# First mixer: queries and keys projected with head dimensions on the partitions

## The chip, the cores and the metric

The program runs on one NeuronCore of a Trainium2 chip. The metric is the device time of one execution, in microseconds (us), the median of a few runs. It computes two transformer blocks one after the other in f32 for 512 tokens of width 1024. The change lies in the first block's mixer, which is the first fifth of the span.

## The reference

The mixer projects the normalised input and turns queries and keys by a rotary angle, per head of 64 dimensions, in two halves of 32:

```python
proj = jnp.einsum('bsd,de->bse', xn, w_in)
q_a, k_a, v_a, q_r, k_r, v_r, g_r, gate_logits = jnp.split(proj, IN_SPLIT_POINTS, axis=-1)

def apply_rotary(t, cos, sin):
    t1, t2 = jnp.split(t.astype(jnp.float32), 2, axis=-1)
    return jnp.concatenate([t1 * c - t2 * s, t1 * s + t2 * c], axis=-1)
```

There are 24 attention heads, in 3 groups of 8. Group 0 attends in a window of neighbouring tokens, groups 1 and 2 with dilations 4 and 16, so their tokens are taken apart by their place modulo 4. The three groups' outputs are mixed by a softmax over their log-sums. Beside attention there are 8 retention heads (queries and keys of 64, values of 128, a gate g_r through silu) and 16 blocks of 128 gate logits through a sigmoid. The attention part and the retention part, each through its own branch matrix, are gated, added and projected; after that come a mixture of 64 experts and the whole second block, which the change doesn't touch.

## The kernel before, in words

SBUF holds one arena. `m.aT` is the normalised input with the model dimension on the partitions: 8 slices `m.aT[:, k, :]` of 128 x 512 tokens. Weights come in 28 chunks into a ring of three slots (`m.ring`), loaded by SyncE in the order of use.

The list `STEPS` sets the order of the whole mixer; every engine walks through it. A step projects one piece into one of two PSUM banks, `banks[s % 2]`, in turn:
- "A" (48 steps: 4 head pairs q, 3 groups g, 4 token tiles t): 128 tokens of queries, keys and values of two heads, 384 columns, as 8 matmuls over k. The stationary operand is a slice of `m.aT` of 128 tokens, for dilated groups every fourth token (`m.aT[:, k, t::4]`); the moving operand is the weight, 384 wide (line 429).
- "R1" and "R2" (32 steps): the same for two retention heads: queries, keys and the first head's values; then the second head's values and both gates.
- "G" (16 steps): 128 gate logits, with the weight stationary and all 512 tokens moving (line 425).

Of an A or R1 step, ScalarE copies the values out. Queries and keys lie there with tokens on the partitions: VectorE multiplies by cosine and sine (lines 629 to 631), GpSimd adds (line 752), and one step later TensorE turns the result by two transposes (line 438), which ScalarE copies to `m.qk` or `m.rqk` (line 544).

Between projections stand units, two for each head pair, at the steps in `UNITS`: an attention unit makes scores (line 450), VectorE masks them and takes maxima, ScalarE the exponentials (line 554) one step later, TensorE transposes them two steps later (line 472, copied by line 564) and multiplies them by the values three steps later (line 484). A retention unit makes scores (line 463), VectorE multiplies them by a table of decays that GpSimd made (lines 760 and 761, line 669), TensorE multiplies by the values one step later (line 498), and VectorE and GpSimd normalise and gate.

An engine waits by counting semaphores: `proj_done` counts finished projections, `proj_read` and `rope_read` the reads that let a bank be used again, `qk_ready` the finished queries and keys. Every engine executes in the order of its own loop, so a wait holds up all that stands behind it.

SyncE's queue carries, besides the chunks, the reorder of attention outputs through DRAM and an exchange of retention queries and keys between partition halves (`m.rqs`). It issues in order: a wait ahead of one transfer delays all later ones. The weights of later stages stand behind those of the mixer.

Of the kernel before, what the change touches and what calls it, by code (L numbers as in the profile page):

```python
# [7 lines left out]
ALU = mybir.AluOpType  # L8
# [3 lines left out]
P = 128  # L12
# [45 lines left out]
def constants():  # L58

    p = np.arange(P)[:, None]  # L60
    c = np.arange(WB)[None, :] - WOFF
    t = {}
    t["ident"] = np.eye(P)
    inv = (1.0 / (np.float32(10000.0) ** (np.arange(0, HD, 2, dtype=np.float32) / np.float32(HD)))).astype(np.float32)
    ang = (np.arange(S, dtype=np.float32)[:, None] * inv[None, :]).astype(np.float32)
    cos, sin = np.cos(ang.astype(np.float64)), np.sin(ang.astype(np.float64))
    t["cos"] = cos.reshape(T, P, HD // 2).transpose(1, 0, 2).reshape(P, -1)
    t["sin"] = sin.reshape(T, P, HD // 2).transpose(1, 0, 2).reshape(P, -1)
    t["nsin"] = -t["sin"]
    for name in ("cos", "sin"):  # L70
        x = cos if name == "cos" else sin
        t[name + "4"] = x.reshape(P, T, HD // 2).reshape(P, -1)
    t["nsin4"] = -t["sin4"]
# [98 lines left out]
MIX_STEPS = {12 * (q + 1) + 14: q for q in range(4)}  # L172


def chunk_no(s):

    return s // 4 if s < 80 else 20 + (s - 80) // 2
# [4 lines left out]


def rope_steps():
    return [s for s, x in enumerate(STEPS) if x[0] in ("A", "R1")]
# [45 lines left out]
def mixer_memory(arena):  # L231
# [3 lines left out]
    m.cos, m.sin, m.nsin = (sp(T, HD // 2) for _ in range(3))  # L235
    m.cos4, m.sin4, m.nsin4 = (sp(T, HD // 2) for _ in range(3))
    m.trig = Space(arena, at)(6 * T * HD // 2)
# [17 lines left out]
    m.ra = [sp(4, 2, HD // 2) for _ in range(2)]  # L255
    m.rb = [sp(4, 2, HD // 2) for _ in range(2)]
    m.rot = [sp(2 * HP2) for _ in range(2)]
# [34 lines left out]
    "proj_done", "rope_read", "rot_ready", "proj_read", "t_done", "qk_ready", "s_done",  # L292
# [54 lines left out]
def first_of_mixer(sp, A, m, G):  # L347

    consts = A["consts"]
    cols, _ = const_columns()  # L350
    for t in range(T):
        sp.wait_ge(G[f"x_in{t}"], 16)
    for i, name in enumerate(("ret_decay_fwd", "ret_decay_bwd")):
        sp.dma_start(m.decay[:, i, :], A[name][0].partition_broadcast(P)).then_inc(G["tables_in"], 16)
    sp.dma_start(m.trig, consts[:, cols["cos"][0]:cols["cos"][0] + 6 * T * HD // 2])\
# [11 lines left out]
def sp_mixer(sp, A, m, G, by_token):  # L367
    need = Need(sp)
    for c in range(N_CHUNK):
        if c < NSLOT:  # L370
            continue
        if c >= NSLOT:
# [12 lines left out]
            if c % 2 == 0 and 0 <= hp < 4:  # L385
                need(G["qk_ready"], 48 + 4 * (hp + 1))
                need(G["s_done"], ATT_BANKS * len(ATT_UNITS))
                if hp >= 2:
# [12 lines left out]
ROPES = [s for s, x in enumerate(STEPS) if x[0] in ("A", "R1")]  # L401


def ropes_to(s):

    return sum(r <= s for r in ROPES)

# [5 lines left out]
def pe_mixer(nc, pe, m, G, banks):  # L413
    need = Need(pe)
    for s in range(NSTEP):

        if s < NPROJ:
            kind, a, b, t = STEPS[s]
# [3 lines left out]
            w = m.ring[c % NSLOT]  # L422
            for k in range(KT):
                if kind == "G":
                    ins = pe.matmul(banks[s % 2][:, :], w[:, k, tile(b)], m.aT[:, k, :],
                                    start=(k == 0), stop=(k == KT - 1))
                else:
                    rows = m.aT[:, k, t::4] if kind == "A" and b else m.aT[:, k, tile(t)]
                    ins = pe.matmul(banks[s % 2][:, 0:CW], rows, w[:, k, :],  # L429
                                    start=(k == 0), stop=(k == KT - 1))  # L430
            ins.then_inc(G["proj_done"], 1)

        if s - 1 in ROPES:
            n = ROPES.index(s - 1)
            need(G["rot_ready"], n + 1)
            need(G["qk_ready"], n)
# [17 lines left out]
        if u and u[0] == "ret":  # L454
            _, hp, k, _ = u
            r, rows = RET_UNITS.index(u), slice(RK * k, RK * k + RK)
            need(G["qk_ready"], 48 + 4 * (hp + 1))
# [18 lines left out]
        if u and u[0] == "att":  # L476
# [3 lines left out]
            need(G["proj_read"], 12 * (q + 1))  # L480
# [9 lines left out]
        if u and u[0] == "ret":  # L490
# [4 lines left out]
            need(G["proj_read"], 48 + 8 * (hp + 1))  # L495
# [7 lines left out]
def act_mixer(nc, act, A, m, G, banks):  # L503
    need = Need(act)
    step = Tick(act, G["act_step"])
    for s in range(NSTEP):
        if s < NPROJ:
            kind, a, b, t = STEPS[s]
            bank = banks[s % 2]
            need(G["proj_done"], s + 1)  # L510
            if kind in ("A", "R1"):
                need(G["rope_read"], ropes_to(s))
            if kind == "A":
                need(G["pv_done"], 2 * (a - 1))
                act.activation(m.v[a % 2][:, t, b, :], bank[:, 2 * HP2:3 * HP2], ACT.Copy)\
                   .then_inc(G["proj_read"], 1)
            if kind == "R1":
                need(G["ro_done"], 2 * (a - 1))
                act.activation(m.rv[a % 2][:, t, tile(0)], bank[:, 2 * P:3 * P], ACT.Copy)\
                   .then_inc(G["proj_read"], 1)  # L520
            if kind == "R2":
                need(G["ry_ready"], 2 * (a - 1))
                act.activation(m.rv[a % 2][:, t, tile(1)], bank[:, 0:P], ACT.Copy)
                act.activation(m.rg[a % 2][:, t, :], bank[:, P:3 * P], ACT.Silu)\
                   .then_inc(G["proj_read"], 1)
# [7 lines left out]
        if s - 1 in ROPES:  # L533
            n = ROPES.index(s - 1)
            kind, a, b, t = STEPS[s - 1]
            need(G["t_done"], n + 1)
            src = banks[2][:, 0:2 * P].rearrange("p (i c) -> p i c", i=2)
            if kind == "A":
                need(G["s_done"], 2 * ATT_BANKS * (a - 1))
                dst = m.qk[a % 2][:, b, :, tile(t)]  # L540
            else:
                need(G["rs_done"], 8 * (a - 1))
                dst = m.rqk[a % 2][:, :, tile(t)]
            act.activation(dst, src, ACT.Copy).then_inc(G["qk_ready"], 1)
# [47 lines left out]
def dve_mixer(nc, dve, m, G, banks):  # L592
# [23 lines left out]
    for sn in range(NSTEP):  # L616

        if sn < NPROJ and sn in ROPES:
            n = ROPES.index(sn)
            t = STEPS[sn][3]  # L620
            x = banks[sn % 2][:, 0:2 * HP2].rearrange("p (h two d) -> p h two d", h=4, two=2)
            need(G["proj_done"], sn + 1)
            need(G["rot_ready"], n - 1)
            by4 = STEPS[sn][0] == "A" and STEPS[sn][2] > 0
            cos, sin, nsin = (m.cos4, m.sin4, m.nsin4) if by4 else (m.cos, m.sin, m.nsin)
            cos = cos[:, t, :].unsqueeze(1).unsqueeze(1).broadcast_to([P, 4, 2, HD // 2])
            sin = sin[:, t, :].unsqueeze(1).broadcast_to([P, 4, HD // 2])
            nsin = nsin[:, t, :].unsqueeze(1).broadcast_to([P, 4, HD // 2])
# [113 lines left out]
def pool_mixer(nc, pool, A, m, G):  # L742
# [4 lines left out]
    for s in range(NSTEP):  # L747
        if s < NPROJ and s in ROPES:
            n = ROPES.index(s)
            need(G["rope_read"], n + 1)  # L750
            need(G["t_done"], n - 1)
            pool.tensor_tensor(m.rot[n % 2], m.ra[n % 2].rearrange("p a b c -> p (a b c)"),  # L752
                               m.rb[n % 2].rearrange("p a b c -> p (a b c)"), ALU.add)\
                .then_inc(G["rot_ready"], 1)
# [9 lines left out]
        if u and u[0] == "ret":  # L764
# [6 lines left out]
            need(G["proj_read"], 48 + 8 * (hp + 1))  # L771
# [2559 lines left out]
```

## Time and profile before

| | us |
|---|---|
| median of 3 runs (3159.18 to 3166.43) | 3160.93 |
| span of the profiled execution | 3162.3 |
| of it TensorE busy | 2834.0 |
| VectorE, ScalarE, GpSimd busy | 1071.4, 487.1, 659.1 |
| first mixer's projections (line 429), busy | 432.0 |
| gate projections (line 425), busy | 110.9 |

The span goes from the first to the last instruction of one execution. Busy times of one engine may hide waits that follow each other, and a matmul's record is longer than the distance to the next one, because matmuls overlap: the distance between starts is what counts. A matmul and the load of its stationary operand (PEld) are recorded apart; a load of the next matmul runs beside the present one.

### The profile page before, as it was taken

How to read it: one execution, taken by the hardware profiler on the slowest of the kernel's cores; microseconds unless marked ns; L12 is line 12 of the kernel's file. 1: busy time of each engine (PE TensorE's matmuls, PEld its weight loads, DVE VectorE, ACT ScalarE, POOL GpSimd, SP SyncE). 2: the span in 40 equal slices, each digit the busy share in tenths (PEclk: the TensorE clock that was granted, in tenths of full speed). 3: DMA queues.
4: the chain of work that ended last, by engine and by line, in shares of the span. 5: the costliest groups of instructions: out<-in, count | busy, mean ns of one | idle time of the engine just before them, and what ended most of it. 6: DMA issues, size and time to landing. Idle time of an engine off the chain costs nothing.

```text
span 3162.3 us, 32461 instructions
## 1 busy us (share of the span) xinstructions
PE 2834.0 (90%) x13294; PEld 1762.6 (56%) x13294; DVE 1071.4 (34%) x2331; ACT 487.1 (15%) x1116; POOL 659.1 (21%) x543
## 2 busy tenths in 40 slices
PE   8999999999986766766766799999999999999998
PEld 7888766544852322322322365558874565488853
DVE  2222222101142122122122143465554335365554
ACT  1222332210100000000000032221110214111100
POOL 1111023301100000000000020055547300265554
PEclk9999999999988888888888899999999999999999
DMA  4121121121399999999999922223330222233210
GB/s 167 61 74 63 65 87 53 60 84 50 146 380 427 428 428 427 428 427 428 427 427 423 398 100 74 67 80 114 119 113 0 90 81 89 65 113 106 95 60 27
DMA packets 136406, 581.39 MB, mean 184 GB/s; under 512 B 16314, under 2 KB 87482, under 8 KB 108226
## 3 DMA queue, kind: packets, MB, share of 16 engines
q1 hardware_dynamic: 136258, 579.30, 46.6%
q8 instruction: 107, 1.75, 0.2%
q14 instruction: 41, 0.34, 0.0%
HBM read 569.75 MB, written 4.28 MB: 182 GB/s over the span
## 4 chain that ended last, share of the span: by engine, by line
PE 49%; DMA 20%; DVE 2%; issue 1%; ACT 1%; SPq 0%; POOL 0%; POOLq 0%; DVEq 0%
DMA arena<-in_moe_w 19%; PE bank L2846 15%; PE bank L1335 9%; PE bank L2161 8%; PE bank L2874 7%; PE bank L2362 3%; PE bank L2825 2%; DMA arena<-in_w_down 1%; PE bank L2313 1%; PE bank L2302 0%; PE bank L2291 0%; SPq L1164 0%; PE bank L1982 0%; PE bank L1358 0%; PE bank L2317 0%
## 5 line engine op out<-in xcount | busy, mean ns | idle before, releaser
L1335 PE MATMUL bank<-arena 128*32 128x512 f32 x2048 | 290.2, 729 | 234.4 <-DMA arena<-in_moe_w 234.4
L2846 PE MATMUL bank<-arena 128*128 128x256 f32 x2240 | 484.9, 378 | 0.1
L2846 PEld LDWEIGHTS bank<-arena 128*128 128x128 f32 x2240 | 424.0, 189 | 61.7 <-issue 1.4
L429 PE MATMUL bank<-arena 128*128 128x384 f32 x1280 | 432.0, 490 | 1.0 <-PEq L856 1.0
L429 PEld LDWEIGHTS bank<-arena 128*128 128x128 f32 x1280 | 298.0, 238 | 105.9 <-issue 6.2
L1335 PEld LDWEIGHTS bank<-arena 128*32 128x32 f32 x2048 | 79.9, 131 | 443.7 <-issue 443.0
L2980 POOL TENSOR_TENSOR arena<-arena 128x512 f32<-128x512 f32 x200 | 259.0, 1307 | 195.0 <-PE bank L2846 194.7
L2874 PE MATMUL bank<-arena 128*128 128x512 f32 x616 | 265.7, 592 | 1.6 <-DMA arena<-in_w_down 1.6
L2161 PE MATMUL bank<-arena 128*128 128x512 f32 (+3 forms) x736 | 255.3, 502 | 5.6 <-ACT arena L2446 4.1
L2049 POOL TENSOR_TENSOR arena<-arena 128x1 f32<-128x1 f32 x20 | 11.3, 566 | 1123.7 <-DVE arena L3186 941.1
L2874 PEld LDWEIGHTS bank<-arena 128*128 128x128 f32 x616 | 116.2, 189 | 148.5 <-issue 147.2
L2161 PEld LDWEIGHTS bank<-arena 128*128 128x128 f32 x736 | 137.7, 191 | 103.2 <-issue 64.8
L1638 DVE TENSOR_TENSOR arena<-bank,arena 64x512 f32<-64x512 f32 x32 | 33.6, 1051 | 430.4 <-ACT arena L1443 430.4
L2999 POOL TENSOR_TENSOR arena<-arena 128x512 f32<-128x512 f32 x110 | 148.5, 1354 | 97.0 <-PE bank L2874 51.8
L1358 PE MATMUL bank<-arena 128*32 128x512 f32 x1024 | 120.9, 614 | 20.9 <-ACT arena L1451 17.1
L629 DVE TENSOR_TENSOR arena<-bank,arena 128x256 f32<-128x256 f32 x64 | 27.2, 426 | 310.5 <-PE bank L429 310.5
L752 POOL TENSOR_TENSOR arena<-arena 128x256 f32<-128x256 f32 x64 | 46.7, 729 | 380.9 <-DVE arena L631 380.9
L1284 PEld LDWEIGHTS bank<-arena 128*128 128x128 f32 x1024 | 117.2, 194 | 14.9 <-issue 12.6
L1284 PE MATMUL bank<-arena 128*128 128x128 f32 x1024 | 120.2, 278 | 2.1 <-DVE arena L1564 2.1
L1443 ACT ACTIVATE arena<-bank 64x512 f32<-64x512 f32 x32 | 18.9, 591 | 640.7 <-PE bank L1335 640.7
L1298 PE MATMUL bank<-arena 64*128 64x512 f32 x512 | 114.3, 595 | 0.9 <-DVE arena L1644 0.9
L2362 PE MATMUL bank<-arena 128*128 128x512 f32 x256 | 111.9, 592 | 1.4 <-ACT arena L2481 1.4
(333 smaller groups left out, 3070.0 us busy)
## 6 DMA issues: line engine op xcount, KB each, us to landing
arena<-in_moe_w SPq DMA_DIRECT2D x188, 2048.0 KB, 23.2
arena<-in_w_up SPq DMA_DIRECT2D x44, 1024.0 KB, 7.7
arena<-in_w_in SPq DMA_DIRECT2D x22, 1536.0 KB, 6.9
arena<-in_w_down SPq DMA_DIRECT2D x6, 2048.0 KB, 7.8
arena<-in_w_in SPq DMA_DIRECT2D x8, 1024.0 KB, 5.6
arena<-in_moe_w SPq DMA_DIRECT2D x8, 1024.0 KB, 19.8
arena<-in_w_in SPq DMA_DIRECT2D x4, 2048.0 KB, 9.7
arena<-in_w_out SPq DMA_DIRECT2D x4, 2048.0 KB, 7.9
```

The costliest lines, as they stand in the source:

```text
L429: ins = pe.matmul(banks[s % 2][:, 0:CW], rows, w[:, k, :], start=(k == 0), stop=(k == KT - 1))
L1284: ins = pe.matmul(banks[5 + d // 4][:, tile(d % 4)], m.hn[:, t, tile(d)], m.G[:, t, :], start=(t == 0), stop=(t == T - 1))
L1298: ins = pe.matmul(scatter_bank(banks, t, half, last)[:, :], m.gt[pr][rows, tile(t)], m.yo[pr][rows, :], start=(pr == 0), stop=(pr == 1))
L1335: ins = pe.matmul(banks[pr][q:q + CAP, :], m.xt[:, k, c:c + CAP], up_view(m, slots[2 * e2 + up])[:, k, :], start=(k == 0), stop=(k == KT - 1))
L1358: ins = pe.matmul(banks[3 + pr][q:q + CAP, :], m.ht[:, f, CAP * e2:CAP * e2 + CAP], down_view(m, slots[4 + e2])[:, f, 512 * half:512 * hal ...
L2161: ins = pe.matmul(out, a, b, start=(i == 0), stop=(i == len(terms) - 1))
L2362: ins = pe.matmul(row_banks(banks, 2 * l + 1, t)[half][:, :], m.mixT[:, k, tile(t)], slot_view(m, i)[:, k, :], start=(first and k == ks[0] ...
L2825: ins = pe.matmul(banks[2 * (j % 2) + half][:, part], w[:, k, c0:c0 + P], m.aT[:, k, part], start=(k == 0), stop=(k == KT - 1))
L2846: ins = pe.matmul(out, weights[:, k, :], rows[:, k, :], start=(k == 0), stop=(k == KT // 2 - 1))
L2874: ins = pe.matmul(banks[seven_banks(i) + u][:, :], rows[:, tile(u)], weights, start=(n == 0), stop=(n == NPAIR - 1))
L2980: pool.tensor_tensor(m.wsum[g % len(m.wsum)], up_weights(m, l, j, *a), up_weights(m, l, j, *b), SIGN[op])\
L2999: pool.tensor_tensor(m.bsum[g % len(m.bsum)], down_weights(m, l, p, *a), down_weights(m, l, p, *b), SIGN[op])\
```

## The change

Queries and keys are projected with the weight stationary and the 512 tokens moving, so head dimensions lie on the partitions at once. An A step of before becomes, per head pair and group, one step for 128 query dimensions, one for 128 key dimensions and one for values; the retention steps become RQ, RK, two RV and two RG. For dilated groups the 512 moving tokens are taken in the order of their classes, every fourth one. Values and retention gates keep the tokens stationary, now against 128 columns of weights at a time. The transposes go.

The rotary turn is done on the transposed layout: VectorE multiplies the bank by cosine, ScalarE copies the bank into `m.swapped` with the halves of 32 partitions exchanged (four copies), GpSimd multiplies that by signed sine in place and adds the two. `m.by_cos` and `m.swapped` exist once. The tables are stored by dimension, 2 x 512 columns instead of 6 x 128. Units move to the matching steps of the shorter list (76 instead of 96).

```diff
-STEPS = ([("A", q, g, t) for q in range(4) for g in range(AG) for t in range(T)]
-         + [(k, hp, 0, t) for hp in range(4) for k in ("R1", "R2") for t in range(T)]
-         + [("G", j // 2, j % 2, 0) for j in range(16)])
+STEPS = ([(k, q, g) for q in range(4) for g in range(AG) for k in ("AQ", "AK", "AV")]
+         + [x for hp in range(4) for x in (("RQ", hp, 0), ("RK", hp, 0), ("RV", hp, 0),
+                                           ("RV", hp, 1), ("RG", hp, 0), ("RG", hp, 1))]
+         + [("G", j // 2, j % 2) for j in range(16)])
...
-            out[12 * (q + 1) + 2 + 5 * hh] = ("att", q, hh, 0)
+            out[QSTEP * (q + 1) + 4 * hh] = ("att", q, hh, 0)
...
-            out[48 + 8 * (hp + 1) + 3 + 3 * k] = ("ret", hp, k, 0)
+            out[RSTEP + HSTEP * (hp + 1) + 2 + 3 * k] = ("ret", hp, k, 0)
...
+def in_classes(x):
+    return x.rearrange("p (i t) -> p t i", t=T)
+def in_tiles(x):
+    return x.rearrange("p (t i) -> p t i", t=T)
...
 # TensorE
-            need(G["proj_read"], s - 1)
+            need(G["proj_read"], copies_to(s - 2))
+            need(G["swapped"], ropes_to(s - 2))
+            w = m.ring[c % NSLOT][:, :, tile(column_block(s))]
+            out = banks[s % 2]
+            if kind[-1] in "QKG" and kind != "RG":
+                for k in range(KT):
+                    tokens = in_classes(m.aT[:, k, :]) if kind[0] == "A" and b else in_tiles(m.aT[:, k, :])
+                    ins = pe.matmul(in_tiles(out), w[:, k, :], tokens, start=(k == 0), stop=(k == KT - 1))
+            else:
+                for t in range(T):
+                    for k in range(KT):
+                        rows = m.aT[:, k, t::4] if kind[0] == "A" and b else m.aT[:, k, tile(t)]
+                        ins = pe.matmul(out[:, tile(t)], rows, w[:, k, :], start=(k == 0), stop=(k == KT - 1))
...
-            for i in range(2):
-                ins = pe.transpose(banks[2][:, tile(i)], m.rot[n % 2][:, tile(i)], m.ident)
...
 # ScalarE
+            if kind[1:] in ("Q", "K"):
+                need(G["by_cos"], ROPES.index(s) + 1)
+                need(G["qk_ready"], ROPES.index(s))
+                for i in range(4):
+                    j = i ^ 1
+                    ins = act.activation(m.swapped[32 * i:32 * i + 32, :], bank[32 * j:32 * j + 32, :], ACT.Copy)
+                ins.then_inc(G["swapped"], 1)
...
+                act.activation(m.v[a % 2][:, :, b, :], in_tiles(bank), ACT.Copy).then_inc(G["proj_read"], 1)
...
 # VectorE
-            dve.tensor_tensor(m.ra[n % 2], x, cos, ALU.mult)
-            dve.tensor_tensor(m.rb[n % 2][:, :, 0, :], x[:, :, 1, :], nsin, ALU.mult)
-            dve.tensor_tensor(m.rb[n % 2][:, :, 1, :], x[:, :, 0, :], sin, ALU.mult)\
-               .then_inc(G["rope_read"], 1)
+            need(G["qk_ready"], ROPES.index(sn))
+            turn = in_classes if STEPS[sn][0][0] == "A" and STEPS[sn][2] else in_tiles
+            dve.tensor_tensor(in_tiles(m.by_cos), in_tiles(banks[sn % 2]), turn(m.cosT), ALU.mult)\
+               .then_inc(G["by_cos"], 1)
...
 # GpSimd
+            turn = in_classes if kind[0] == "A" and b else in_tiles
+            step.wait(step(pool.tensor_tensor(in_tiles(m.swapped), in_tiles(m.swapped), turn(m.sinT), ALU.mult)))
+            need(G["by_cos"], n + 1)
+            pool.tensor_tensor(dst, m.by_cos, m.swapped, ALU.add).then_inc(G["qk_ready"], 1)
...
 # SyncE, ahead of the exchange of retention halves
+                if hp:
+                    need(G["rs_done"], 8 * (hp - 1) + 1)
```

## Rows read from the trace of the kernel before

**Rows 1.** The page: busy us (share of the span), instructions; granted clock in 40 slices.
```profile
PE 2834.0 (90%) x13294; PEld 1762.6 (56%) x13294; DVE 1071.4 (34%) x2331; ACT 487.1 (15%) x1116; POOL 659.1 (21%) x543
...
PEclk9999999999988888888888899999999999999999
```
**Rows 2.** Busy time by stretch of the mixer: us, PE, PEld, DVE, ACT, POOL busy, PEclk, DMA.
```profile
88.16:174.01 85.85, 83.72 (x374) 70.00 (x373) 17.33 (x91) 23.50 (x88) 8.74 (x12) 1.00 0.18 63
...
sum 674.37, PE 661.39 PEld 463.04 DVE 149.84 ACT 166.62 POOL 110.25; mean PE 94.48 PEld 66.15 DVE 21.41 ACT 23.80 POOL 15.75
```
**Rows 3.** Waits from 22.6 to 697 us: total, times, longest.
```profile
DVE arena L629 <- PE bank L429: 310.5, 59, 11.6
...
DVE arena L669 <- POOL arena L761: 69.2, 8, 24.2
...
PE bank L472 <- ACT arena L554: 10.3, 8, 3.1
```
**Rows 4.** SyncE's issues from 640 us: start, us, engine, line.
```profile
697.12 0.39 SPq L1003 DMA_DIRECT2D arena<-in_w_attn_branch  x1
...
848.48 2.63 SPq L1164 DMA_DIRECT2D arena<-in_moe_w  x5
```
**Rows 5.** The chain that ended last, in the first expert stage: start, us.
```profile
922.87 16.87 DMA arena<-in_moe_w
```
**Rows 6.** Timeline, TensorE's projection steps: start us, us, engine, line, count.
```profile
60.59 5.46 PE L429 MATMUL bank<-arena 128*128 128x384 f32 x16
...
66.10 5.46 PE L429 MATMUL bank<-arena 128*128 128x384 f32 x16
...
88.16 5.34 PE L429 MATMUL bank<-arena 128*128 128x384 f32 x16
...
93.55 5.34 PE L429 MATMUL bank<-arena 128*128 128x384 f32 x16
```
**Rows 7.** Line 429, loads of a contiguous step (88.2 to 92.9): ns min/median/max.
```profile
L429 PEld LDWEIGHTS bank<-arena x16: 188/190/192, 88.1 to 92.7; 128*128 128x128 f32 x16
```
**Rows 8.** Line 429, loads of a dilated step (60.6 to 65.5): ns min/median/max.
```profile
L429 PEld LDWEIGHTS bank<-arena x16: 307/308/332, 60.5 to 65.2; 128*128 128x128 f32 x16
```
**Rows 9.** Timeline at 33.30 us: behind two transposes, contiguous tokens.
```profile
33.16 0.30 PEld L429 LDWEIGHTS bank<-arena 128*128 128x128 f32 x2
...
33.26 0.49 PE L429 MATMUL bank<-arena 128*128 128x384 f32 x1
```
**Rows 10.** Timeline at 60.72 us: behind two transposes, every fourth token.
```profile
60.48 0.54 PEld L429 LDWEIGHTS bank<-arena 128*128 128x128 f32 x2
...
60.59 0.61 PE L429 MATMUL bank<-arena 128*128 128x384 f32 x1
```
**Rows 11.** Timeline, ScalarE after two gate steps that follow each other.
```profile
654.97 0.69 ACT L531 ACTIVATE arena<-bank,arena 128x512 f32<-128x512 f32 x1 [6.18 <-PE bank L425]
661.84 0.69 ACT L531 ACTIVATE arena<-bank,arena 128x512 f32<-128x512 f32 x1 [6.18 <-PE bank L425]
```
**Rows 12.** Timeline, loads ahead of the matmuls with the values, 64 columns each.
```profile
126.15 4.10 PEld L484 LDWEIGHTS bank<-arena 128*128 128x128 f32 x36
```
**Rows 13.** Groups by line and shape: busy us, mean ns, idle before.
```profile
L1063 DVE TENSOR_TENSOR arena<-bank,arena 128x512 f32<-128x512 f32 x16 | 11.1, 693 | 133.9 <-PE bank L1033 133.9
...
L926 DVE SCALAR_TENSOR_TENSOR arena<-arena 128x1024 f32<-128x1024 f32 x4 | 8.1, 2032 | 4.1 <-POOL arena L900 4.1
L930 DVE SCALAR_TENSOR_TENSOR arena<-arena 128x1024 f32<-128x1024 f32 x4 | 4.9, 1279 | 9.7 <-DMA arena<-in_norm_mix_w 9.7
...
L564 ACT ACTIVATE arena<-bank 128x512 f32<-128x512 f32 x32 | 16.9, 611 | 1.8 <-PE bank L472 1.8
...
L773 POOL TENSOR_TENSOR arena<-arena 128x512 f32<-128x512 f32 x8 | 10.2, 1277 | 13.5 <-DVE arena L691 13.5
```
**Rows 14.** Timeline of one attention unit: first and last of its exponentials.
```profile
113.86 0.51 ACT L554 ACTIVATE arena<-arena 128x256 f32<-128x256 f32 x1
...
118.47 0.19 ACT L554 ACTIVATION_READ_ACCUMULATOR arena<-arena 128x1 f32 x1
```

More of the change, by code:

```diff
@@ L69, in constants @@
     t["nsin"] = -t["sin"]
[L70 to L73, printed above, removed]
+    t["cosT"] = np.tile(cos.T, (4, 1))
+    t["sinT"] = np.concatenate([-sin.T, sin.T] * 2, axis=0)
     near = np.arange(3 * P)[None, :] - P - p
@@ L97, in const_columns @@
     return out, at
-STEPS = ([("A", q, g, t) for q in range(4) for g in range(AG) for t in range(T)]
-         + [(k, hp, 0, t) for hp in range(4) for k in ("R1", "R2") for t in range(T)]
-         + [("G", j // 2, j % 2, 0) for j in range(16)])
+STEPS = ([(k, q, g) for q in range(4) for g in range(AG) for k in ("AQ", "AK", "AV")]
+         + [x for hp in range(4) for x in (("RQ", hp, 0), ("RK", hp, 0), ("RV", hp, 0),
+                                           ("RV", hp, 1), ("RG", hp, 0), ("RG", hp, 1))]
+         + [("G", j // 2, j % 2) for j in range(16)])
 NPROJ = len(STEPS)
+QSTEP, HSTEP = 3 * AG, 6
+RSTEP = 4 * QSTEP
+GSTEP = RSTEP + 4 * HSTEP
+NA_ROPE = 4 * AG * 2
 def units():
@@ L169, in results, with column_block @@
     return m.o0[q % 2] if g == 0 else m.o4[:, :, g - 1, :, :]
-MIX_STEPS = {12 * (q + 1) + 14: q for q in range(4)}
+MIX_STEPS = {QSTEP * (q + 1) + 10: q for q in range(4)}
 def chunk_no(s):
-    return s // 4 if s < 80 else 20 + (s - 80) // 2
+    return s // 3 if s < GSTEP else 20 + (s - GSTEP) // 2
+def column_block(s):
+    return s % 3 if s < GSTEP else (s - GSTEP) % 2
 N_CHUNK = 28
 NSLOT = 3
-def rope_steps():
-    return [s for s, x in enumerate(STEPS) if x[0] in ("A", "R1")]
 HP2 = 2 * HD
@@ L234, in mixer_memory @@
     at = sp.at
-    m.cos, m.sin, m.nsin = (sp(T, HD // 2) for _ in range(3))
-    m.cos4, m.sin4, m.nsin4 = (sp(T, HD // 2) for _ in range(3))
-    m.trig = Space(arena, at)(6 * T * HD // 2)
+    m.cosT, m.sinT = sp(S), sp(S)
+    m.trig = Space(arena, at)(2 * S)
     m.tabs = sp(3, WB)
@@ L254, in mixer_memory @@
     m.e12 = sp(2, WB)
-    m.ra = [sp(4, 2, HD // 2) for _ in range(2)]
-    m.rb = [sp(4, 2, HD // 2) for _ in range(2)]
-    m.rot = [sp(2 * HP2) for _ in range(2)]
+    m.by_cos, m.swapped = sp(S), sp(S)
     m.negm = sp(AG, T, 2)
@@ L291 @@
 MIXER_SEMS = [
-    "proj_done", "rope_read", "rot_ready", "proj_read", "t_done", "qk_ready", "s_done",
+    "proj_done", "by_cos", "swapped", "proj_read", "qk_ready", "s_done",
     "negm_ready", "exp_done", "pt_done", "pt_ready", "pv_done", "att_out", "att_sent", "att_in",
@@ L354, in first_of_mixer @@
         sp.dma_start(m.decay[:, i, :], A[name][0].partition_broadcast(P)).then_inc(G["tables_in"], 16)
[L355 removed]
+    sp.dma_start(m.trig, consts[:, cols["cosT"][0]:cols["cosT"][0] + 2 * S])\
       .then_inc(G["tables_in"], 16)
@@ L400, with copies_to @@
 NSTEP = NPROJ + 2
-ROPES = [s for s, x in enumerate(STEPS) if x[0] in ("A", "R1")]
+ROPES = [s for s, x in enumerate(STEPS) if x[0][1:] in ("Q", "K")]
+def in_classes(x):
+    return x.rearrange("p (i t) -> p t i", t=T)
+def in_tiles(x):
+    return x.rearrange("p (t i) -> p t i", t=T)
 def ropes_to(s):
     return sum(r <= s for r in ROPES)
+def copies_to(s):
+    return max(s + 1, 0) - ropes_to(s)
 def att_index(u):
@@ L417, in pe_mixer @@
         if s < NPROJ:
-            kind, a, b, t = STEPS[s]
+            kind, a, b = STEPS[s]
             c = chunk_no(s)
             need(G[f"w_in{c % NSLOT}"], mload_count(c))
-            need(G["proj_read"], s - 1)
[L422 to L430, printed above, removed]
-            ins.then_inc(G["proj_done"], 1)
[L433 to L436, printed above, removed]
-            for i in range(2):
-                ins = pe.transpose(banks[2][:, tile(i)], m.rot[n % 2][:, tile(i)], m.ident)
-            ins.then_inc(G["t_done"], 1)
+            need(G["proj_read"], copies_to(s - 2))
[11 more added lines that the diff above has]
+                        ins = pe.matmul(out[:, tile(t)], rows, w[:, k, :], start=(k == 0), stop=(k == KT - 1))
+            ins.then_inc(G["proj_done"], 1)
         u = UNITS.get(s)
@@ L444, in pe_mixer @@
             a = att_index(u)
-            need(G["qk_ready"], 12 * (q + 1))
+            need(G["qk_ready"], 2 * AG * (q + 1))
             need(G["att_out"], a)
@@ L456, in pe_mixer @@
             r, rows = RET_UNITS.index(u), slice(RK * k, RK * k + RK)
-            need(G["qk_ready"], 48 + 4 * (hp + 1))
+            need(G["qk_ready"], NA_ROPE + 2 * (hp + 1))
             need(G["att_out"], len(ATT_UNITS))
@@ L479, in pe_mixer @@
             need(G["pt_ready"], ACHUNK * (a + 1))
-            need(G["proj_read"], 12 * (q + 1))
+            need(G["proj_read"], copies_to(QSTEP * (q + 1) - 1))
             for i, (h, g, t, _, _, ks) in enumerate(in_banks(part)):
@@ L494, in pe_mixer @@
             need(G["rn_ready"], r)
-            need(G["proj_read"], 48 + 8 * (hp + 1))
+            need(G["proj_read"], copies_to(RSTEP + HSTEP * (hp + 1) - 1))
             for t in range(T):
@@ L507, in act_mixer @@
         if s < NPROJ:
-            kind, a, b, t = STEPS[s]
+            kind, a, b = STEPS[s]
             bank = banks[s % 2]
             need(G["proj_done"], s + 1)
-            if kind in ("A", "R1"):
-                need(G["rope_read"], ropes_to(s))
-            if kind == "A":
+            if kind[1:] in ("Q", "K"):
[5 more added lines that the diff above has]
+                ins.then_inc(G["swapped"], 1)
+            if kind == "AV":
                 need(G["pv_done"], 2 * (a - 1))
-                act.activation(m.v[a % 2][:, t, b, :], bank[:, 2 * HP2:3 * HP2], ACT.Copy)\
-                   .then_inc(G["proj_read"], 1)
-            if kind == "R1":
+                act.activation(m.v[a % 2][:, :, b, :], in_tiles(bank), ACT.Copy).then_inc(G["proj_read"], 1)
+            if kind == "RV":
                 need(G["ro_done"], 2 * (a - 1))
-                act.activation(m.rv[a % 2][:, t, tile(0)], bank[:, 2 * P:3 * P], ACT.Copy)\
-                   .then_inc(G["proj_read"], 1)
-            if kind == "R2":
+                act.activation(m.rv[a % 2][:, :, tile(b)], in_tiles(bank), ACT.Copy).then_inc(G["proj_read"], 1)
+            if kind == "RG":
                 need(G["ry_ready"], 2 * (a - 1))
-                act.activation(m.rv[a % 2][:, t, tile(1)], bank[:, 0:P], ACT.Copy)
-                act.activation(m.rg[a % 2][:, t, :], bank[:, P:3 * P], ACT.Silu)\
-                   .then_inc(G["proj_read"], 1)
+                act.activation(m.rg[a % 2][:, :, tile(b)], in_tiles(bank), ACT.Silu).then_inc(G["proj_read"], 1)
             if kind == "G":
@@ L616, in dve_mixer @@
     for sn in range(NSTEP):
[L618 to L621, printed above, removed]
+        if sn in ROPES:
             need(G["proj_done"], sn + 1)
[L623 to L628, printed above, removed]
-            dve.tensor_tensor(m.ra[n % 2], x, cos, ALU.mult)
-            dve.tensor_tensor(m.rb[n % 2][:, :, 0, :], x[:, :, 1, :], nsin, ALU.mult)
-            dve.tensor_tensor(m.rb[n % 2][:, :, 1, :], x[:, :, 0, :], sin, ALU.mult)\
-               .then_inc(G["rope_read"], 1)
+            need(G["qk_ready"], ROPES.index(sn))
+            turn = in_classes if STEPS[sn][0][0] == "A" and STEPS[sn][2] else in_tiles
+            dve.tensor_tensor(in_tiles(m.by_cos), in_tiles(banks[sn % 2]), turn(m.cosT), ALU.mult)\
+               .then_inc(G["by_cos"], 1)
         u = UNITS.get(sn)
@@ L747, in pool_mixer @@
     for s in range(NSTEP):
-        if s < NPROJ and s in ROPES:
+        if s in ROPES:
             n = ROPES.index(s)
[L750 to L754, printed above, removed]
+            kind, a, b = STEPS[s]
+            i = "QK".index(kind[1])
+            need(G["swapped"], n + 1)
+            if kind[0] == "A":
+                need(G["s_done"], 2 * ATT_BANKS * (a - 1))
+                dst = m.qk[a % 2][:, b, i, :]
+            else:
+                need(G["rs_done"], 8 * (a - 1))
+                dst = m.rqk[a % 2][:, i, :]
+            turn = in_classes if kind[0] == "A" and b else in_tiles
+            step.wait(step(pool.tensor_tensor(in_tiles(m.swapped), in_tiles(m.swapped), turn(m.sinT), ALU.mult)))
+            need(G["by_cos"], n + 1)
+            pool.tensor_tensor(dst, m.by_cos, m.swapped, ALU.add).then_inc(G["qk_ready"], 1)
         u = UNITS.get(s + 1)
@@ L770, in pool_mixer @@
             need(G["rn_ready"], r + 1)
-            need(G["proj_read"], 48 + 8 * (hp + 1))
+            need(G["proj_read"], copies_to(RSTEP + HSTEP * (hp + 1) - 1))
             need(G["smalls_in"], 32)
```

14 lines of the change are left out of this document (1 added, 13 removed).

## The prediction

> **What bounds the kernel now.** I read the page first, then the busy time by stage, the waits of the first mixer, the queue of SyncE, and single projection steps. The page shows TensorE busy 90% of the span at a clock that stays at its upper level in the first quarter [rows 1]. The stage table shows the same for the first mixer: from 22.63 to 697 us TensorE is busy 661.4 of 674.4 us at a granted clock of 1.00 in the stretch shown (2.4 GHz, the higher of its two levels) [rows 2]. The waits say that the helpers wait for TensorE: VectorE sits idle 310.5 us for the projection's matmuls, while TensorE waits for ScalarE's exponentials 10.3 us in all [rows 3]. So a microsecond of TensorE there is a microsecond of the stage. It is passed on whole: SyncE issues the branch weights at 697.12 us, as the mixer ends, and the first expert weights only at 848.48 us [rows 4]; from then on the chain of waits is paced by these transfers [rows 5], which start later when the mixer ends later.
>
> The sum goes against the profiled execution: its span of 3162.3 us is 1.4 us above the median of the runs, 3160.93, and inside their spread. I add the difference to the median.
>
> **What TensorE does in a projection step.** Each f32 matmul is two instructions (16 in a step of 8) [rows 6], each with its own weight load, which runs beside the matmul ahead of it.
> - Before, 384 columns: a step on contiguous tokens takes 5.39 us from start to start (88.16 to 93.55) with its two transposes, a step on every fourth token 5.51 (60.59 to 66.10) [rows 6].
> - 512 contiguous columns: gate steps follow one another every 6.87 us (654.97 to 661.84), 16 instructions, 0.429 each [rows 11].
> - 128 columns or fewer with a new contiguous load each: 36 loads in 4.10 us, less the last one's length (0.19, rows 7), over 35 = 0.112 each [rows 12].
>
> **Strided loads, the cost that was hidden.** A load of aT[:, k, t::4] takes every fourth f32. Its record is 308 ns at the median, against 190 for contiguous tokens [rows 7, 8]. Where the matmul ahead has 384 columns this is covered. Behind the short transposes it is not: with contiguous tokens the load is issued at 33.16 and its matmul starts at 33.26, 0.106 us later, and lasts 0.49 [rows 9]; with strided tokens the load is issued at 60.48, and the matmul, recorded from 60.59, lasts 0.61, 0.12 longer [rows 10]. A strided load therefore takes between twice 0.107 (0.213) and 0.107 + 0.121 (0.228). I take 0.220.
>
> **Attention: what goes and what comes (4 head pairs, 3 groups, the last two dilated).** Removed: 16 contiguous steps at 5.39 and 32 dilated at 5.51, 86.2 + 176.3 = 262.5 us, with the transposes. Added:
> - Queries and keys of group 0: 8 steps of 16 x 0.429, 54.9 us.
> - Values of group 0: 4 steps of 64 instructions (4 token tiles, 8 k, 2 halves), 128 columns wide: 256 x 0.112 = 28.7 us.
> - Values of groups 1 and 2: 8 x 64 = 512 instructions. The strided load now stands ahead of a matmul of 128 columns, so it sets the pace: 512 x 0.220 = 112.6 us (109.1 to 116.7).
> - Queries and keys of groups 1 and 2: 16 steps, 256 instructions. The tokens are now the moving operand, read every fourth f32 (512 of them). No row of before has such a matmul. Lower end: it streams as if contiguous, 0.429 (below that there is no reason: it is the same number of columns). Upper end: each column pays what a strided load pays, 0.121/128 us, so 0.429 + 0.484 = 0.913. VectorE's rows lie between: the norm that scatters its output takes 2032 ns, the contiguous one 1279, 1.59 times [rows 13]. The nearest row is the load: the same engine, the same tokens, the same stride, and at 0.107 per 128 columns the same pace as a matmul (0.429 per 512); it is slowed to double. I take 2 x 0.427 + 0.002 = 0.856: 256 x 0.856 = 219.1 us (109.8 to 233.7).
>
> Sum: 54.9 + 28.7 + 112.6 + 219.1 = 415.3, so **+152.8 us**.
>
> The Trainium skill (SBUF — State Buffer, section Specifications (TRN2)) says that SBUF is organised in 16-byte lines and that full bandwidth needs at least two hits in a line; every fourth f32 has one. The load rows agree. By this rule the moving operand pays too, which is the value taken. The same skill (TensorE: Matmul & The Clock Gate, section Step-by-step: what each phase is for) says that the moving operand and the weights come through two independent read ports; if the slow port were the weights' alone, the sum would be that of the second rival. No run so far shows which.
>
> **Retention and gates.** Removed: 16 steps with transposes at 5.39 and 16 without at 5.18 (two contiguous 128-column instructions at 0.107 less): 169.1. Added: 8 steps of 6.87 (54.9) and 16 steps of 64 x 0.112 (114.7), all contiguous: 169.6. **+0.5 us.** Gate steps are unchanged.
>
> **Stalls on ScalarE.** The exponentials of an attention unit take from 113.86 to 118.66, 4.8 us [rows 14]; TensorE has one projection step to cover them and now waits 1.3 us for each of 8 units [rows 3]. After the change the first unit of a pair has a key step ahead: VectorE's cosine product 0.69, four ScalarE copies at 0.61 at most [rows 13], 4.8 and some 0.3 of signals, 8.2 us, against a value step of 7.15 (64 x 0.112): 1.1 us, four times. The second unit has a copy of 0.61 ahead and a query step of 6.87 us or more as cover: next to nothing. Some 5 us instead of 10.3: **-5 us** (-8 to +2).
>
> **The rotary chain itself.** Per step: VectorE 0.69 (1.10 where the table is read strided, by VectorE's ratio), ScalarE 2.0 to 2.4, GpSimd 1.28 (2.04) and 1.28 [rows 13], signals 0.6 (an estimate): 6 to 7.6 us. TensorE needs only ScalarE's last read, two steps later, and each pair of chains (at most 15.2 us) has three steps, 20.9 us in group 0 and over 41 in the dilated ones, so it hides; without that cover it costs what exceeds 20.9. Queued behind the new waits are ScalarE's value copies and exponentials, counted above, and GpSimd's decay tables, for which VectorE waits 69.2 us already [rows 3] while TensorE goes on with the next projection step: 2.6 us of products and sums ahead of them use up part of that step's 7.15. SyncE's exchange of the retention halves waits for one more signal, three steps (21 us) ahead of its reader. The table transfer grows by a third of 0.4 MB; at the start TensorE is released by its own transposes.
>
> **Total: +152.8 + 0.5 - 5 = +148 us, 3160.9 + 148 = 3309 us.** With the ends of the unknown costs (109.1 to 116.7; 0.853 to 0.913, that is 218.4 to 233.7; stalls -8 to +2): +140 to +175, 3301 to 3336.
>
> **Rivals.**
> - *Reading slow for weights alone*: the moving operand streams at 0.429. Queries and keys of groups 1 and 2 cost 109.8: 306.0 - 262.5 = +43.5, less 5: 3199. For it: only loads are seen slowed. Against: loads and matmuls show the same contiguous pace, so the same narrow supply.
> - *Moving operand slowed less than double*, as VectorE's 1.59: 0.682, 174.6 us, 3264.
> - *Dilated reads hidden (the other side)*: the engine fetches far enough ahead that both keep pace, 512 x 0.112 and 256 x 0.429: 250.9, -11.6, less 5: 3144. It decides from a margin of 17 us: dilated values under 0.145 (0.112 + 17/512), or dilated queries under 0.495. Against it: the 0.12 us that one strided load already costs behind a short matmul.
> - *The chain becomes the bound*: with both strided readers at three times their contiguous time (2.1 and 3.8) a chain is near 10 us, and where units interleave some 2 us per dilated pair are lost, 8 x 2 to 3 us on top: 3330.
>
> **Chances.** Doubled moving operand 0.66; less than double 0.10; weights alone 0.17; chain 0.03; hidden 0.04. Time 3309, range 3192 to 3336 (it must reach the weights-alone case to leave out under 2 in 10). Only the hidden case can be faster by over 0.2% (what a measurement here can tell from no change), and a quarter of it lies within 0.2%: faster 0.03, same 0.01, slower 0.96.
>
> **What would show it.** Start to start of dilated 512-column matmuls: 0.86 (right), 0.43 (weights alone), 0.68 (between). Dilated 128-column matmuls: 0.22, against 0.112 for group 0. The mixer's last gate at 696 us moves to about 845, the first expert weights from 848 to about 996, and nothing later changes. TensorE's wait for the exponentials falls from 10.3 to about 5 us, and it has no wait for ScalarE's exchange copies. I am wrong if dilated values run near 0.112, or if TensorE stands idle for the rotary chain.

## The result and the profile after

The changed kernel takes 3321.12 us (median of 4 runs, 3320.57 to 3323.18) against 3163.43 for the kernel before in the same comparison: a ratio of 1.0499, 95% interval 1.0485 to 1.0512, 157.7 us slower. The forecast was 148 us slower; the direction was right, and the time lies in the stated range.

The page of the changed kernel, TensorE's line and the granted clock in 40 slices, answers to [rows 1]:

```profile
PE 2997.5 (90%) x14190; PEld 1811.1 (55%) x14190; DVE 1052.1 (32%) x2171; ACT 531.9 (16%) x1110; POOL 698.6 (21%) x543
...
PEclk9999999999999888888888899999999999999999
```

TensorE is busy 163.5 us longer and its share is the same; VectorE is relieved by 19 us, which buys nothing, as it had been waiting for TensorE [rows 3]. The clock is at its upper level wherever the mixer runs. The busy times from the first projection to the last gate step answer to [rows 2] (length, PE, PEld, DVE, ACT, POOL, clock, DMA share, GB/s):

```profile
22.42:856.80 834.38, 829.21 (x3504) 511.59 (x3504) 130.69 (x470) 210.91 (x466) 149.47 (x113) 1.00 0.16 54
```

Busy TensorE time grows from 661.4 to 829.2 us (+167.8), its idle time falls from 674.4 - 661.4 = 13.0, of which 0.8 lie behind the last gate step, to 5.2. SyncE's issues show that the whole of it is passed on, answering to [rows 4]:

```profile
857.97 0.39 SPq L1004 DMA_DIRECT2D arena<-in_w_attn_branch  x1
...
1007.91 3.17 SPq L1165 DMA_DIRECT2D arena<-in_moe_w  x5
```

The branch weights are issued 160.9 us later, the first expert weights 159.4, and the span ends 156.5 later (3318.8 against 3162.3). The first expert transfers pace the chain as before [rows 5]:

```profile
1080.09 17.26 DMA arena<-in_moe_w
```

Where the time went is seen in TensorE's timeline (start, length, line, count; line 446 projects queries and keys, line 451 values):

```profile
22.42 13.97 PE L446 MATMUL bank<-arena 128*128 128x512 f32 x32 [0.99 <-PEq L857]
36.23 7.31 PE L451 MATMUL bank<-arena 128*128 128x128 f32 x64
43.38 28.97 PE L446 MATMUL bank<-arena 128*128 128x512 f32 x32
72.17 14.97 PE L451 MATMUL bank<-arena 128*128 128x128 f32 x64
86.97 28.97 PE L446 MATMUL bank<-arena 128*128 128x512 f32 x32
```

Each pair of rows is one group of the first head pair. Starts are what counts: group 0 takes 13.81 us for queries and keys and 7.15 for values, group 1 takes 28.79 and 14.80. So a dilated instruction of 512 columns stands 28.79/32 = 0.900 us apart from the next, a dilated one of 128 columns 14.80/64 = 0.231. The records of single instructions of group 1 (ns min/median/max) say which part is long, values first:

```profile
L451 PE MATMUL bank<-arena x57: 397/397/397, 72.7 to 85.8; 128*128 128x128 f32 x57
L451 PEld LDWEIGHTS bank<-arena x57: 330/330/330, 72.8 to 85.9; 128*128 128x128 f32 x57
```

```profile
L446 PE MATMUL bank<-arena x16: 1062/1078/1080, 43.4 to 56.9; 128*128 128x512 f32 x16
L446 PEld LDWEIGHTS bank<-arena x15: 207/208/209, 44.3 to 56.9; 128*128 128x128 f32 x15
```

The same for queries and keys of group 0, whose tokens are contiguous:

```profile
L446 PE MATMUL bank<-arena x32: 592/592/667, 22.4 to 35.8; 128*128 128x512 f32 x32
```

For values the load is the long one (190 with contiguous tokens [rows 7]); for queries and keys the load is nearly as short as ever, and the matmul itself lasts 1078 instead of 592. Both operands pay when they are the strided one. TensorE's waits in the mixer, answering to [rows 3]:

```profile
PE bank L485 <- ACT arena L556: 5.2, 5, 1.3
PE bank L446 <- PEq L857: 1.0, 1, 1.0
```

The exponentials cost 5.2 us instead of 10.3. These two rows are all of TensorE's waits there: the rotary chain is not among them.

### The profile page after: what moved, and what is told of

The parts are those of the page before. It is cut to its first block, busy times and chain, and to the rows that moved or that the text cites. A ratio compares the mean times of both kernels' runs of the same rounds, so it can differ in the third digit from the quotient of the medians.

```text
span 3318.8 us, 33939 instructions
## 1 busy us (share of the span) xinstructions
PE 2997.5 (90%) x14190; PEld 1811.1 (55%) x14190; DVE 1052.1 (32%) x2171; ACT 531.9 (16%) x1110; POOL 698.6 (21%) x543
## 4 chain that ended last, share of the span: by engine, by line
PE 46%; DMA 19%; DVE 1%; issue 1%; ACT 1%; SPq 0%; POOL 0%; POOLq 0%; DVEq 0%
DMA arena<-in_moe_w 18%; PE bank L2847 15%; PE bank L1336 9%; PE bank L2162 7%; PE bank L2875 7%; PE bank L2363 3%; PE bank L2826 2%; DMA arena<-in_w_down 1%; PE bank L2314 0%; PE bank L2303 0%; PE bank L2292 0%; SPq L1165 0%; PE bank L1983 0%; PE bank L2318 0%; PE bank L1359 0%
## 5 line engine op out<-in xcount | busy, mean ns | idle before, releaser
L446 PE MATMUL bank<-arena 128*128 128x512 f32 x768 | 457.0, 755 | 1.0 <-PEq L857 1.0
L2847 PEld LDWEIGHTS bank<-arena 128*128 128x128 f32 x2240 | 424.0, 189 | 61.7 <-issue 1.4
L2981 POOL TENSOR_TENSOR arena<-arena 128x512 f32<-128x512 f32 x200 | 259.2, 1309 | 194.8 <-PE bank L2847 194.5
L446 PEld LDWEIGHTS bank<-arena 128*128 128x128 f32 x768 | 147.3, 195 | 275.6 <-issue 275.1
L451 PEld LDWEIGHTS bank<-arena 128*128 128x128 f32 x1792 | 265.0, 231 | 8.7 <-issue 8.2
L451 PE MATMUL bank<-arena 128*128 128x128 f32 x1792 | 267.2, 310 | 0.0
L2875 PE MATMUL bank<-arena 128*128 128x512 f32 x616 | 265.7, 592 | 1.3 <-DMA arena<-in_w_down 1.3
L2875 PEld LDWEIGHTS bank<-arena 128*128 128x128 f32 x616 | 116.2, 189 | 148.1 <-issue 145.7
L2162 PEld LDWEIGHTS bank<-arena 128*128 128x128 f32 x736 | 137.0, 190 | 101.9 <-issue 63.6
L624 DVE TENSOR_TENSOR arena<-bank,arena 128x512 f32<-128x512 f32 x32 | 28.3, 885 | 450.2 <-PE bank L446 450.2
L3000 POOL TENSOR_TENSOR arena<-arena 128x512 f32<-128x512 f32 x110 | 148.5, 1355 | 96.6 <-PE bank L2875 51.4
L753 POOL TENSOR_TENSOR arena<-arena 128x512 f32<-128x512 f32 x32 | 44.8, 1401 | 516.5 <-ACT arena L529 516.5
L529 ACT ACTIVATE arena<-bank 32x512 f32<-32x512 f32 x128 | 75.5, 590 | 314.7 <-DVE arena L624 241.9
L1285 PEld LDWEIGHTS bank<-arena 128*128 128x128 f32 x1024 | 115.5, 192 | 14.9 <-issue 12.6
```

What stands on the lines that cost most here:

```text
L446: ins = pe.matmul(in_tiles(out), w[:, k, :], tokens, start=(k == 0), stop=(k == KT - 1))
L451: ins = pe.matmul(out[:, tile(t)], rows, w[:, k, :], start=(k == 0), stop=(k == KT - 1))
L529: ins = act.activation(m.swapped[32 * i:32 * i + 32, :], bank[32 * j:32 * j + 32, :], ACT.Copy)
L1285: ins = pe.matmul(banks[5 + d // 4][:, tile(d % 4)], m.hn[:, t, tile(d)], m.G[:, t, :], start=(t == 0), stop=(t == T - 1))
L2162: ins = pe.matmul(out, a, b, start=(i == 0), stop=(i == len(terms) - 1))
L2847: ins = pe.matmul(out, weights[:, k, :], rows[:, k, :], start=(k == 0), stop=(k == KT // 2 - 1))
```

## Experiments

**Theory**: the whole loss is the stride of four f32, at the moving operand of queries and keys (256 instructions) and at the loads of the values (512). **Rivals**: the 512-column or the 128-column form itself is slow; the chain over VectorE, ScalarE and GpSimd sets the pace.

The changed kernel and the runs below were measured in three comparisons, in which the kernel before had medians of 3163.4, 3165.6 and 3165.8 us; times of different comparisons can be set against each other to about 2 us.

### One stride taken away at a time

Queries and keys with tokens in plain order:

```diff
-                    tokens = in_classes(m.aT[:, k, :]) if kind[0] == "A" and b else in_tiles(m.aT[:, k, :])
+                    tokens = in_tiles(m.aT[:, k, :])
```

> The changed kernel with the moving tokens of all queries and keys read in plain order (it leaves out the sorting of groups 1 and 2 into classes there; values and tables as changed). Theory (every fourth f32 is read at less than half pace as moving operand): the 256 dilated instructions fall from 0.900 to 0.429 us, 120.6 us less than 3321, about 3200. Rival (the 0.900 comes from the 512-column matmul that follows a load, or from the bank's pattern, not from the stride): about 3321, no change.

Values with tokens in plain order:

```diff
-                        rows = m.aT[:, k, t::4] if kind[0] == "A" and b else m.aT[:, k, tile(t)]
+                        rows = m.aT[:, k, tile(t)]
```

> The changed kernel with the stationary tokens of the values read in plain order (it leaves out the sorting into classes there). Theory (a strided load sets the pace of 128-column matmuls): 512 instructions fall from 0.233 to 0.112 us, 62 us less, about 3259. Rival (the loads still pull ahead and only the queries cost): 3321.

Measured 3201.97 us (ratio to the kernel before 1.0115, 1.0098 to 1.0132) and 3260.26 us (1.0300, 1.0283 to 1.0317): 119 and 61 us below the changed kernel, against 120.6 and 62 expected. SyncE's issue of the branch weights marks the mixer's end; it comes 120.5 and 61.1 us earlier than at 857.97:

```profile
737.48 0.39 SPq L1004 DMA_DIRECT2D arena<-in_w_attn_branch  x1
796.84 0.39 SPq L1004 DMA_DIRECT2D arena<-in_w_attn_branch  x1
```

The timeline of the first, groups 0 and 1:

```profile
22.34 13.97 PE L446 MATMUL bank<-arena 128*128 128x512 f32 x32 [0.99 <-PEq L857]
36.15 7.31 PE L451 MATMUL bank<-arena 128*128 128x128 f32 x64
43.29 13.90 PE L446 MATMUL bank<-arena 128*128 128x512 f32 x32
57.03 14.97 PE L451 MATMUL bank<-arena 128*128 128x128 f32 x64
71.83 13.90 PE L446 MATMUL bank<-arena 128*128 128x512 f32 x32
```

Queries and keys of group 1 take 57.03 - 43.29 = 13.74 us, as in group 0, while the values keep their 14.80. In the second it is the other way round:

```profile
44.27 28.96 PE L446 MATMUL bank<-arena 128*128 128x512 f32 x32
73.05 7.33 PE L451 MATMUL bank<-arena 128*128 128x128 f32 x64
80.21 25.36 PE L446 MATMUL bank<-arena 128*128 128x512 f32 x28
```

The two costs are separate and add up to 180 us, more than the whole loss of 157.7. So without strides the change should win.

### Both taken away: a sorted copy

A second copy of the input, in class order, in space that retention uses only later; ScalarE and GpSimd write it beside the first three projection steps:

```diff
+    m.aT4 = Space(arena, m.rqk_at)(KT, S)
...
+            if s == 3:
+                need(G["class_act"], 1)
+                need(G["class_pool"], 1)
...
+                    tokens = in_tiles((m.aT4 if kind[0] == "A" and b else m.aT)[:, k, :])
...
+                        rows = (m.aT4 if kind[0] == "A" and b else m.aT)[:, k, tile(t)]
...
+    for k in range(4):
+        ins = act.activation(in_tiles(m.aT4[:, k, :]), in_classes(m.aT[:, k, :]), ACT.Copy)
+    ins.then_inc(G["class_act"], 1)
...
+    for k in range(4, KT):
+        ins = pool.tensor_copy(in_tiles(m.aT4[:, k, :]), in_classes(m.aT[:, k, :]))
+    ins.then_inc(G["class_pool"], 1)
```

> The changed kernel with a second copy of the input, sorted into the four classes once at the mixer's start (four slices by ScalarE, four by GpSimd, beside the first three projection steps), and all reads of groups 1 and 2 from that copy. Theory (the strides are the whole loss): 120.6 + 62 us less, about 3138 to 3146, which is 15 to 25 below the kernel before, as transposes and some waits are gone. Rival (with steps of 6.9 us the rotary chain becomes the bound, or the copies delay the first steps): at or above the 3163 of the kernel before.

Measured 3142.23 us (3141.39 to 3145.42), ratio to the kernel before 0.9928, 0.9912 to 0.9945: faster than both kernels, inside the expected band. Its timeline:

```profile
22.24 13.97 PE L450 MATMUL bank<-arena 128*128 128x512 f32 x32 [0.99 <-PEq L867]
36.05 7.31 PE L455 MATMUL bank<-arena 128*128 128x128 f32 x64
43.19 13.93 PE L450 MATMUL bank<-arena 128*128 128x512 f32 x32
56.95 7.31 PE L455 MATMUL bank<-arena 128*128 128x128 f32 x64
64.10 13.93 PE L450 MATMUL bank<-arena 128*128 128x512 f32 x32
```

All groups now take 20.9 us. The copies are done long before step 3 needs them at 43.19 (GpSimd's below; ScalarE's four end at 27.77):

```profile
22.25 4.31 POOL L748 COPY arena<-arena 128x512 f32<-128x512 f32 x4
```

### The kernel before without its strides

```diff
-                    rows = m.aT[:, k, t::4] if kind == "A" and b else m.aT[:, k, tile(t)]
+                    rows = m.aT[:, k, tile(t)]
```

> The kernel before with its stationary tokens read in plain order (it leaves out the sorting into classes). Theory (behind a matmul of 384 columns a strided load is covered, and only the first of each of 32 dilated steps shows 0.12 us): 3.8 us less, about 3159.5, near the limit of what can be told from no change; in the trace a dilated step falls from 5.51 to 5.39. Rival (strided loads also slow the matmuls beside them): clearly more than 4 us less.

Measured 3162.75 us against 3165.6, ratio 0.9992, 0.9983 to 1.0002: the run time can't tell it from no change. The traces can. The branch weights are issued 3.7 us earlier than at 697.12 [rows 4], against 3.8 expected, and a step that took 5.51 us [rows 6] takes 65.10 - 59.70 = 5.40:

```profile
59.70 5.34 PE L429 MATMUL bank<-arena 128*128 128x384 f32 x16
64.88 0.38 PE L438 MATMUL bank<-arena 128*128 128x128 f32 x2
65.10 5.34 PE L429 MATMUL bank<-arena 128*128 128x384 f32 x16
...
693.38 0.39 SPq L1003 DMA_DIRECT2D arena<-in_w_attn_branch  x1
```

So 384 columns did cover the strided loads before: as many strided loads (512) cost under 4 us there and 61 in the changed kernel.

### Other strides

```diff
+                    n = {0: 1, 1: 2, 2: 8}[b] if kind[0] == "A" else 1
+                    tokens = m.aT[:, k, :].rearrange("p (i t) -> p t i", t=n)
...
+                        if kind[0] == "A" and b == 1:
+                            rows = m.aT[:, k, t % 2 + 2 * P * (t // 2):2 * P * (t // 2) + 2 * P:2]
...
```

> The changed kernel with other strides (it leaves out the sorting into four classes): in group 1 every second token, moving for queries and keys and stationary for values; in group 2 every eighth token moving, every fourth stationary. Theory (the cost is one read of a 16-byte line for each f32, as the Trainium skill's SBUF page has it, so what matters is whether two elements share a line): every second token runs at 0.429 for 512 columns and 0.112 for 128, every eighth at 0.900 like every fourth; in all 8 x 16 x 0.471 + 4 x 64 x 0.121 = 91 us less, about 3230. Rival (any step over one costs): every second token at or above 0.6 us. Second rival (the cost grows with the distance): every eighth clearly above 0.9.

A single run, 3240.6 us against about 3230 expected. Group 1 (every second token), then group 2's queries and keys (every eighth), up to its values:

```profile
43.85 14.56 PE L447 MATMUL bank<-arena 128*128 128x512 f32 x32
58.25 7.69 PE L456 MATMUL bank<-arena 128*128 128x128 f32 x64
65.78 29.56 PE L447 MATMUL bank<-arena 128*128 128x512 f32 x32
95.16 10.07 PE L456 MATMUL bank<-arena 128*128 128x128 f32 x43
```

Every second f32: 14.40/32 = 0.450 for 512 columns and 7.53/64 = 0.118 for 128, 5% above contiguous. Every eighth: 29.38/32 = 0.918, 2% above every fourth. The jump in cost lies between steps of two and four; beyond it distance hardly matters, below it the stride hardly does. Both rivals of this run's expectation fall. A step of three was not run, so these runs don't tell a line of 16 bytes from another limit between 8 and 16 bytes. The theory was too clean by those 5% and 2%: the mixer ends 84 us earlier instead of 91 (branch weights at 773.84), and the two make up 6.5 of the 7 us that are missing.

### Is the chain hidden?

The kernel with the sorted copy, with two more products on GpSimd in each attention chain, and then with six (a 6 in place of the 2):

```diff
+            for _ in range(2 if kind[0] == "A" else 0):
+                step.wait(step(pool.tensor_tensor(m.rn2.rearrange("p a b -> p (a b)"), m.swapped, m.sinT, ALU.mult)))
```

> The kernel with the sorted copy, and two more products by sine on GpSimd in each attention rotary chain (into a buffer that nobody reads). Theory (the chain of some 6 to 7 us hides: a pair of chains has three steps, 20.9 us): 2.7 us more per chain leave two chains at about 18 us, no change from 3142, within 3 us. Rival (the chain already sets some of the steps): 24 chains, up to 65 us more, visibly over 3150.

> The same with six more products: 8 us more per chain, two chains at about 29 us against 20.9 us of steps. Theory: now the chain shows; the first head pair, which has no units between its steps, loses about 8 us in each of three groups, the others, with 18 us of units per pair, a few us each: 30 to 60 us more than 3142. Rival (TensorE needs only ScalarE's read, GpSimd is never waited for): still 3142.

With two: 3139.65 us (3138.93 to 3140.78; ratio to the kernel before 0.9915, 0.9899 to 0.9932), no longer than without them. With six, in a single run: 3194.73 us, 55 more than with two. Its waits of TensorE from 22 to 720 us ("issue": the profile shows nothing that it waited for):

```profile
PE bank L467 <- POOL arena L767: 12.4, 4, 3.8
PE bank L450 <- ACT arena L536: 11.1, 2, 6.1
PE bank L489 <- ACT arena L563: 10.3, 5, 5.3
PE bank L450 <- issue: 4.7, 1, 4.7
```

Only now does TensorE wait for ScalarE's exchange copies (line 536) and for GpSimd's sums ahead of the scores (line 467). Its first dilated groups show the new rhythm:

```profile
49.08 16.98 PE L450 MATMUL bank<-arena 128*128 128x512 f32 x32 [4.67 <-issue]
65.89 7.30 PE L455 MATMUL bank<-arena 128*128 128x128 f32 x64
78.20 16.08 PE L450 MATMUL bank<-arena 128*128 128x512 f32 x32 [5.00 <-ACT arena L536]
```

From 49.08 to 78.20 a group takes 29.1 us, two chains of 14.6, as computed. The cover thus ends between 18 us (the expectation's sum for two products) and 29 us per pair of chains, which fits the 20.9 us of three contiguous steps. Some of the 55 us are no wait: TensorE, now idle between groups, is granted a lower mean clock there. The stretch of the first rows with six products, then the whole mixer with two and with six (length, PE, PEld, DVE, ACT, POOL busy, clock, DMA):

```profile
22.00:130.00 108.00, 90.22 (x361) 53.07 (x360) 18.65 (x56) 23.66 (x38) 73.96 (x60) 0.91 0.20 71
...
22.40:675.60 653.20, 647.11 (x3504) 444.74 (x3504) 133.52 (x470) 216.12 (x471) 214.49 (x165) 1.00 0.21 69
...
23.29:730.20 706.91, 667.35 (x3504) 454.79 (x3504) 139.65 (x470) 216.14 (x471) 337.71 (x261) 0.97 0.19 63
```

The mixer is 53.7 us longer. TensorE's idle time grows from 6.1 to 39.6 us, by 33.5; for the same 3504 matmuls it is busy 20.2 us longer, at a granted clock of 0.97 instead of 1.00.

## Why the prediction was right

- *The bound*: right. Every microsecond of TensorE in the mixer moved the first expert weights (159.4 of 160.9 us) and the end (156.5). The last 3 us are of the size in which runs of the kernel before differ from each other.
- *Dilated values*: 0.220 taken, 0.231 measured: 512 x 0.011 = 6 us too little. The bound 0.107 + 0.121 = 0.228, read from one exposed load [rows 10], was the better value. The same row has it more directly: two strided loads in 0.54 us, less the last one's 0.308 [rows 8], stand 0.23 apart.
- *Dilated queries and keys*: 0.856 taken, 0.900 measured: 11 us too little. Here too the truth lay at the upper end, 0.913, which came from the same exposed load; 0.900 lies inside the bounds given, and the choice of an exact doubling was argued and not read from a row. A strided column costs 0.900/512 = 1.76 ns against 0.84, 2.1 times: more than the doubling I chose.
- *Retention*: +0.5 us, with no term of it seen to be off; its 128-column steps run at 0.112.
- *Stalls*: -5 forecast for the exponentials, -5.1 measured. Idle time fell by 7 in all, because TensorE's wait of 1.8 us ahead of the transposes, which the sum had left out, went with them.
- *The rotary chain*: right. From VectorE's product to GpSimd's sum it takes 5.9 us in group 0 (36.4 to 42.3 us) and 6.5 in a dilated group (58.0 to 64.5), against 6 to 7.6 forecast, and TensorE waits for none of it.
- *Sum*: with the measured 0.900 and 0.231 the terms give 54.9 + 28.7 + 118.3 + 230.4 - 262.5 = +169.8, +0.5, -7: +163, against 160.9 in the trace. Most of the two us that are left is clock. In the kernel before, TensorE stands idle 3.13 us for one unit's exponentials, and right behind that its granted clock is 0.50, the lower of its two levels (1.2 GHz), from 415.5 to 418.5; 18 transposes (line 472) and the 16 matmuls behind them take 3.18 and 5.69 us there from start to start, against 2.02 and 5.17 for the same work at a granted clock of 1.00 (376.44 to 383.63): 1.7 us more. In the changed kernel the longest such wait is 1.3 us and the granted clock of the mixer is 1.00. Rows of the kernel before, the last with its clock ahead of the DMA's columns:

```profile
376.44 2.18 PE L472 MATMUL bank<-arena 128*128 128x128 f32 x18 [0.64 <-ACT arena L554]
378.46 5.34 PE L429 MATMUL bank<-arena 128*128 128x384 f32 x16
383.63 4.12 PE L484 MATMUL bank<-arena 128*128 128x64 f32 x36
...
414.68 3.39 PE L472 MATMUL bank<-arena 128*128 128x128 f32 x18 [3.13 <-ACT arena L554]
417.86 5.85 PE L429 MATMUL bank<-arena 128*128 128x384 f32 x16
423.55 0.38 PE L438 MATMUL bank<-arena 128*128 128x128 f32 x2
...
415.50:418.50 3.00, 3.00 (x14) 2.70 (x13) 0.00 (x0) 2.49 (x5) 0.00 (x0) 0.50 0.02 5
```

- *What was luck*: the two prices were 17 us too low together, and the forecast only 10, because three things that it left out went the other way: the wait ahead of the transposes (1.8 us), this clock (1.7) and the 4 us by which the program's end moved less than the mixer's (156.5 against 160.9).
- *The rule of the Trainium skill*: by the 16-byte lines (SBUF — State Buffer, section Specifications (TRN2)) the moving operand had to pay. The traces agree: it pays, and with other strides it runs at 0.450 where two f32 share such a line and at 0.900 and 0.918 where each has its own. The two read ports, which the Trainium skill names too (TensorE: Matmul & The Clock Gate, section Step-by-step: what each phase is for), did not spare the matmul. The rival that only weights are read slowly put dilated queries and keys at 109.8 us; they take 256 x 0.900 = 230.4.
- *The other side*: the hidden case needed dilated values under 0.145. It was wrong in its mechanism, but its time, 3144, is what the sorted copy reaches (3142), since the copy too leaves no strided read to pay for: the layout was good, the stride was not.
- *Ends of the range*: the ends of the terms add up to +141 and +174; the prediction has +140 and +175, which changes nothing.

## What to carry to other kernels

Before an operand changes its place, from stationary to moving or from a wide matmul to a narrow one, look at its access pattern: here a load of every fourth f32 was nearly free behind a matmul of 384 columns (under 4 us for 512 loads), the same load behind 128 columns set the pace, and a moving operand with that step paid on every column. One exposed instance in the trace prices it; take the price as seen rather than rounded to a neat factor. Where many matmuls read the same strided operand, sort it once on idle engines: 8.5 us of copies beside other work were worth 179 us here.

## What the runs showed that was not expected

- The other engines pay for strides too. VectorE's product with a table read every fourth f32 took 1064 ns against 693, GpSimd's 1522 against 1265. ScalarE's sorted copies took 1126 ns each, against 594 for a contiguous copy of the same size from a bank and 623 for a contiguous silu of that size within SBUF. GpSimd's sorted copies took 1128; no run has a contiguous copy of its own to compare. All of it was covered.
- Reading every second f32 is not quite free either (0.450 against 0.429), and every eighth is slightly dearer than every fourth (0.918 against 0.900). For the moving operand the step and the number of separate passes over the tokens (2, 4, 8) change together, so which of them makes these small differences is not shown.
- Contiguous loads ahead of strided matmuls are recorded longer (208 ns against 190 ns), without effect on the pace, since they stand 900 ns apart.
